# Expert value rows of two token tiles: read as one dense matrix product instead of gathered row by row

## The reference

```
q = xn @ w_q                                   # 8 heads x 2 halves of 128
s1, s2 = scores of each half against 128 keys
top 16 of s1, top 16 of s2, top 16 of their 256 sums -> e = i1*128 + i2   (one of 16384 experts)
g = softmax(top scores)
act = gelu(<u_tab[e], xn>)                     # a row of 2048 of the first table
out = sum over 8 heads x 16 picks of (g * act) * v_tab[e]     # a row of the second table
y = rmsnorm(x + out) * g_final
```

## Time and profile before

| | us |
|---|---|
| runs shown, median of 3 | 4106.34 (4100.68 to 4108.57) |
| the profiled execution, its time | 4110.75 |
| its span, first to last instruction | 4108.9 |
| PE busy / DVE busy / POOL busy | 3168.1 / 2447.8 / 1543.0 |
| mean granted TensorE clock | 0.928 of full |

### The profile page before, as it was taken

The page is one execution under the profiler, slowest core; times in us unless marked ns, Lnnn a source line. Parts: engine busy times, 40 slices in busy tenths (PEclk is TensorE's granted clock), DMA queues, the critical chain, the costliest instruction groups (busy, mean ns, idle before and its releaser), DMA issues.

```text
span 4108.9 us, 35344 instructions
## 1 busy us (share of the span) xinstructions
PE 3168.1 (77%) x11808; PEld 1910.2 (46%) x11808; DVE 2447.8 (60%) x3360; ACT 556.5 (14%) x1113; POOL 1543.0 (38%) x1130
## 2 busy tenths in 40 slices
PE   6999899879878776857915777777777777776776
PEld 5999889775444443535502233232223232322322
DVE  2788810146787775784666565566556555656553
ACT  4444320110010000001000100010011001001100
POOL 2000000014554443552336455445445544554442
PEclk9999999889999998978968999999999999999999
DMA  4322367569999998896879999999999999999997
GB/s 122 89 85 84 104 215 242 190 244 344 391 380 387 385 392 343 333 385 253 342 263 406 409 416 421 421 403 421 414 416 417 422 415 415 418 421 412 422 412 306
DMA packets 406321, 1372.39 MB, mean 334 GB/s; under 512 B 24449, under 2 KB 264065, under 8 KB 264735
## 3 DMA queue, kind: packets, MB, share of 16 engines
q0 software_dynamic: 157584, 1145.05, 68.3%
q1 hardware_dynamic: 246382, 221.85, 16.9%
q10 hardware_dynamic: 2257, 4.40, 0.3%
HBM read 1363.20 MB, written 8.86 MB: 334 GB/s over the span
## 4 chain that ended last, share of the span: by engine, by line
DMA 43%; PE 29%; DVE 14%; issue 9%; POOL 4%; ACT 1%; SPq 0%; DVEq 0%; POOLq 0%; ACTq 0%
DMA region<-in_v_tab_dram,region 29%; DMA region<-in_u_tab_dram,region 13%; PE ps L1366 11%; PE ps L1547 6%; POOL region L527 4%; DVE region L1177 3%; PE ps L1349 3%; PE ps L1351 3%; PE ps L1350 3%; DVE region L1230 2%; DVE region L1168 1%; DVE region L1129 1%; DVE region L1126 1%; DVE region L1128 1%; DVE region L1125 1%
## 5 line engine op out<-in xcount | busy, mean ns | idle before, releaser
L1547 PE MATMUL ps<-region,region 128*128 128x512 f32 x3032 | 1429.1, 621 | 544.0 <-DMA region<-in_v_tab_dram,region 326.8
L1366 PE MATMUL ps<-region,region 128*128 128x160 f32 (+1 forms) x5120 | 1237.2, 404 | 190.4 <-DVE region L1065 57.3
L1230 DVE SCALAR_TENSOR_TENSOR region<-region,region 128x2048 f32<-128x2048 f32 x384 | 876.2, 2291 | 738.8 <-DMA region<-in_u_tab_dram,region 738.8
L527 POOL DMA_INDIRECT region<-in_v_tab_dram,region x544 | 764.3, 1405 | 1268.6 <-PE ps L1547 675.8
L1547 PEld LDWEIGHTS ps<-region,region 128*128 128x128 f32 x3032 | 575.8, 197 | 1397.4 <-issue 1304.3
L1366 PEld LDWEIGHTS ps<-region,region 128*128 128x128 f32 x5120 | 861.1, 196 | 558.9 <-issue 104.1
L527 POOL DMA_INDIRECT region<-in_u_tab_dram,region x544 | 740.7, 1362 | 794.3 <-DVE region L1158 341.0
L1177 DVE SCALAR_TENSOR_TENSOR region<-region,region,region 128x2048 f32<-128x2048 f32 x160 | 376.1, 2351 | 236.8 <-DMA region<-in_v_tab_dram,region 236.6
L1168 DVE SCALAR_TENSOR_TENSOR region<-region,region 128x2048 f32<-128x2048 f32 x160 | 365.3, 2285 | 22.8 <-DMA region<-in_u_tab_dram,region 22.8
L1349 PE MATMUL ps<-region,region 128*128 128x272 f32 x1024 | 297.4, 290 | 0.0
L1351 PE MATMUL ps<-region,region 128*128 128x272 f32 x1024 | 296.4, 289 | 0.0
(11 more groups left out here) (202 smaller groups left out, 1483.2 us busy)
## 6 DMA issues: line engine op xcount, KB each, us to landing
region<-in_w_in_dram SPq DMA_DIRECT2D x192, 512.0 KB
region<-in_w_out_dram SPq DMA_DIRECT2D x64, 512.0 KB
region<-in_w_q_dram SPq DMA_DIRECT2D x64, 512.0 KB
region<-in_w_a_dram SPq DMA_DIRECT2D x32, 512.0 KB
region<-in_w_b_dram SPq DMA_DIRECT2D x32, 512.0 KB
region<-in_u_tab_dram,region POOLq DMA_INDIRECT x544, 14.0
region<-in_v_tab_dram,region POOLq DMA_INDIRECT x544, 14.0
region<-in_x_prompt_dram SPq DMA_DIRECT2D x7, 1024.0 KB, 15.7
```

What stands on the lines that cost most here:

```text
L527: pool.indirect_dma_start(out=slot, out_offset=None, in_=rows_ap, in_offset=bass.IndirectOffsetOnAxis(ap=idx[:, k:k + 1], axis=0)).then_in ...
L1230: stt(out=u_b[s], in0=u_b[s], scalar=1.0, in1=xn_tile(UNITS_A + u), op0=ALU.mult, op1=ALU.mult, accum_out=dots[u % 2][:, k:k + 1]).then_in ...
L1366: last = mm(outs[n][:, 0:WIDTH[g]], wide[s][:, q, n * P:(n + 1) * P], rhs(k), start=(k == 0), stop=(k == n_k - 1))
L1547: last = mm(acc[n][:, b * 512:(b + 1) * 512], diag[:, m, :], v_b[s][:, b * 512:(b + 1) * 512], start=(m == 0), stop=(m == len(rows) - 1))
```

## The change

Group 1's first two tiles (stage 1 of group 1, 256 row steps) gather no value rows. For each token DVE and ACT make one-hot rows from its 128 picks: the upper 7 bits of the expert's number, times the weight (`first_ones`, DVE), and the lower 7 bits (`second_ones`, ACT: 1 - (c - i)^2, cut at 0). PE multiplies the two for one token into a 128x128 block: that token's weights over all 16384 experts. Four tokens are a batch, 32 batches a tile. ACT copies them out of PSUM into `wx` and `wy` (`keep_weights`), 64 KB per partition each. The first tile's batches are spread over the second tile's rows; the second tile's all stand behind 8 row steps of the third. Then SP reads v_tab once, in 128 chunks of 128 rows (1 MB, plain, two slots), and PE multiplies each chunk with both tiles' weights: 8 products of 128x512 per chunk, all accumulated in the 8 banks of PSUM.

The third tile's 128 value rows are gathered and added on DVE, 18 steps behind, while the dense product runs; its u rows then have 2 slots, its value rows 2. Of group 0's 160 value rows, 80 are gathered in its own time and added on DVE, every other step or so; the other 80 are gathered during stage 1, 2 slots, and added on PE by diagonals. The scores of group 1 go to memory and come back unit by unit, since their place is taken. Two memsets at the start (3 and 552 columns) move behind the transposes of the keys, and many regions lie elsewhere. The number of u rows is as before.

```diff
@@ -62,13 +62,25 @@
 ROWS_A = UNITS_A * TOPK
+ROWS_W = 5 * TOPK
+ROWS_1, ROWS_B = 2 * P, 3 * P
 SLOTS_U, SLOTS_V = 3, 2
-TIDY = 19
+VALUE_AT = {V_LAG + v * (ROWS_A - V_LAG) // ROWS_W: v for v in range(ROWS_W)}
+ROWS_P = ROWS_A - ROWS_W
+GROUP_P = 3 * TOPK
+ROW_AT = [m * (ROWS_1 - 2 * TOPK) // ROWS_P for m in range(ROWS_P)]
+BATCH = 4
+BATCHES = P // BATCH
+SPLIT_AT = (P + 4, ROWS_1 + 1)
+BATCH_AT = [[P + 8 + b * (P - 9) // BATCHES for b in range(BATCHES)],
+            [ROWS_1 + 2 + b // 4 for b in range(BATCHES)]]
+ADD_AT = (P + 7, ROWS_1 - 30)
+FOLD_AT, TIDY_AT = ROWS_1 - 26, ROWS_1 - 10
+CHUNKS = 128
+HALF = CHUNKS // 2
+ND = 8
...
@@ -487,13 +513,31 @@
-            for t in range(3):
-                sp.dma_start(xfb[t].rearrange("p (k n) -> p k n", n=P), kept[:, :, t, :]).then_inc(x1_back, 16)
-            sp.dma_start(gfin, g_final.partition_broadcast(P)).then_inc(gfin_in, 16)
+            def kept_rows(t, dst, landed):
+                sp.dma_start(dst.rearrange("p (k n) -> p k n", n=P), kept[:, :, t, :]).then_inc(landed, 16)
+
+            sp.dma_start(gfin[0], g_final.partition_broadcast(P)).then_inc(gfin_in, 16)
+            sp.wait_ge(dot_a, ROWS_A)
+            kept_rows(2, xfz, xz_in)
+            sp.wait_ge(y_ready, 1)
+            sp.dma_start(y_prompt[0, 3 * P:4 * P, :], xf[0]).then_inc(out_p, 16)
+            sp.wait_ge(y_ready, 2)
+            sp.dma_start(xs_out, xf[1][0:TS, :]).then_inc(out_p, 16)
+            sp.wait_ge(v_used, ROWS_P)
+            for c in range(CHUNKS):
+                if c == 1:
+                    sp.wait_ge(built, 2 * BATCHES)
+                if c >= 2:
+                    sp.wait_ge(vt_used, c - 1)
+                sp.dma_start(v_t[c % 2], v_rows[c * P:(c + 1) * P, :]).then_inc(vt_landed[c % 2], 16)
+                if c == HALF + 8:
+                    kept_rows(0, xf[2], xy_in)
+                    kept_rows(1, xf[3], xy_in)
+                    sp.dma_start(gfin[1], g_final.partition_broadcast(P)).then_inc(gfin_again, 16)
+            for n, (row, t) in enumerate(((2 * P, 4), (0, 2), (P, 3))):
+                sp.wait_ge(y_ready, n + 3)
...
@@ -545,47 +591,56 @@
+            def value_row(n):
+                e = n if n < ROWS_A else n + ROWS_1
+                gather(v_rows, v_a[n % SLOTS_V], va_landed[n % SLOTS_V], idx_all, e)
+
+            for p in range(ROWS_A + 1):
                 if p < ROWS_A:
                     if p % TOPK == 0:
                         pool.wait_ge(routed, p // TOPK + 1)
                     if p >= SLOTS_U:
                         pool.wait_ge(dot_a, p - SLOTS_U + 1)
                     gather(u_rows, u_a[p % SLOTS_U], ua_landed[p % SLOTS_U], idx_all, p)
-                v = p - V_AHEAD
-                if v >= 0:
+                if p - 1 in VALUE_AT:
+                    v = VALUE_AT[p - 1]
                     if v >= SLOTS_V:
                         pool.wait_ge(v_added, v - SLOTS_V + 1)
...
+            for r in range(ROWS_1):
+                if r % TOPK == 0:
+                    pool.wait_ge(routed, UNITS_A + r // TOPK + 1)
+                if r == 2:
+                    pool.wait_ge(q_done, 2 * HEADS + 2)
+                if r >= SLOTS:
+                    pool.wait_ge(dot_b, r - SLOTS + 1)
+                gather(u_rows, u_b[r % SLOTS], ub_landed[r % SLOTS], idx_all, ROWS_A + r)
+                for m, at_row in enumerate(ROW_AT):
+                    if at_row == r:
+                        if m < SLOTS_V:
+                            pool.wait_ge(v_added, ROWS_W)
+                        else:
+                            pool.wait_ge(v_used, m - SLOTS_V + 1)
+                        value_row(ROWS_W + m)
+            for z in range(P + V_LAG + 1):
+                if z < P:
+                    r = ROWS_1 + z
+                    if z % TOPK == 0:
+                        pool.wait_ge(routed, UNITS_A + r // TOPK + 1)
+                    pool.wait_ge(dot_b, r - 1)
+                    gather(u_rows, u_b[2 + z % 2], ub_landed[2 + z % 2], idx_all, ROWS_A + r)
+                v = z - V_LAG - 1
+                if v >= 0:
+                    if v < SLOTS_V:
+                        pool.wait_ge(v_used, ROWS_P)
+                    else:
+                        pool.wait_ge(v_added, ROWS_W + v - SLOTS_V + 1)
+                    value_row(ROWS_A + v)
...
@@ -832,13 +894,52 @@
+            def diagonal(m):
+                act.wait_ge(w_ready, (ROWS_W + m) // TOPK + 2)
+                if m >= ND:
+                    act.wait_ge(v_used, m - ND + 1)
+                part(act)
+                nc.scalar.activation(diag[:, m % ND, :], ident, ACT.Copy,
+                                     scale=w_all[:, ROWS_W + m:ROWS_W + m + 1]).then_inc(diag_ready, 1)
+            def second_ones(t, b):
+                n = t * BATCHES + b
+                if n >= 2:
+                    act.wait_ge(built, n - 1)
+                for q in range(BATCH):
+                    last = nc.scalar.activation(one_b[n % 2][:, q, :], count, ACT.Square, scale=-1.0,
+                                                bias=turned[:, 1, BATCH * b + q:BATCH * b + q + 1])
+                last.then_inc(b_square, 1)
+                act.wait_ge(b_square, n + 1)
+                nc.scalar.activation(one_b[n % 2], one_b[n % 2], ACT.Relu, scale=-1.0, bias=ones[:, 0:1]).then_inc(b_ones, 1)
+
+                act.wait_ge(built, n + 1)
+                if t == 0:
+                    nc.scalar.activation(wx[:, :, cols], src, ACT.Copy).then_inc(kept_w, 1)
+                else:
+                    nc.scalar.activation(wy[0][:, :, cols], src[:, 0:HALF], ACT.Copy)
+                    nc.scalar.activation(wy[1][:, :, cols], src[:, HALF:CHUNKS], ACT.Copy).then_inc(kept_w, 1)
...
@@ -866,36 +967,55 @@
             for u in range(UNITS_B):
+                for m, at_row in enumerate(ROW_AT):
+                    if at_row // TOPK == u:
+                        diagonal(m)
+                if u == 2 * HEADS:
+                    turned_copy(1)
+                    act.wait_ge(out_p, 32)
+                    build(1, list(range(BATCHES)))
                 if u < UNITS_B - 1:
                     stage_scores(UNITS_A + u + 1)
                     exponents(UNITS_A + u + 1)
+                if u == HEADS:
+                    turned_copy(0)
+                build(0, [b for b in range(BATCHES) if BATCH_AT[0][b] // TOPK == u])
...
@@ -1220,65 +1343,96 @@
+            def first_ones(t, b):
+                n = t * BATCHES + b
+                dve.wait_ge(turn_read, t + 1)
+                if n >= 2:
+                    dve.wait_ge(built, n - 1)
+                for q in range(BATCH):
+                    col = BATCH * b + q
+                    last = ts_(one_a[n % 2][:, q, :], count, turned[:, 0, col:col + 1], turned[:, 2, col:col + 1],
+                               ALU.is_equal, ALU.mult)
+                last.then_inc(a_ones, 1)
+
...
+            for j in range(2):
+                dve.wait_ge(s_done[j], 2 * HEADS + 1)
+            for r in range(ROWS_B):
+                u, k = divmod(r, TOPK)
+                dot(r)
+                if k == 1:
+                    expert_weights(UNITS_A + u - 1)
+                if k == (12 if u == 2 * HEADS else 3) and u < UNITS_B - 1:
+                    route(UNITS_A + u + 1)
+                    for b in range(BATCHES):
+                        if BATCH_AT[t][b] == r:
+                            first_ones(t, b)
+                if r == ROWS_1 + V_LAG:
+                    dve.wait_ge(xz_in, 16)
+                if r >= ROWS_1 + V_LAG:
+                    value_z(r - ROWS_1 - V_LAG)
+            expert_weights(UNITS_A + UNITS_B - 1)
+            for z in range(P - V_LAG, P):
+                value_z(z)
+            dve.wait_ge(gfin_again, 16)
+            for n in range(2):
+                dve.wait_ge(dense_done, n + 1)
+                tt(xf[2 + n], xf[2 + n], acc[n], ALU.add).then_inc(dense_read, 1)
+            for n in range(2):
+                normalised(slice(2 + n, 3 + n), 6 + n, 1)
...
@@ -1531,28 +1685,71 @@
+            def value_row(m):
+                n = ROWS_W + m
+                first, last_row = m in (0, GROUP_P), m in (GROUP_P - 1, ROWS_P - 1)
+                if m == GROUP_P:
+                    pe.wait_ge(acc_read, 1)
+                pe.wait_ge(diag_ready, m + 1)
+                pe.wait_ge(va_landed[n % SLOTS_V], 16 * (n // SLOTS_V + 1))
+                for b in range(4):
+                    last = mm(acc[0][:, b * 512:(b + 1) * 512], diag[:, m % ND, :],
+                              v_a[n % SLOTS_V][:, b * 512:(b + 1) * 512], start=first, stop=last_row)
+                last.then_inc(v_used, 1)
+
...
+            def batch(t, b):
+                n = t * BATCHES + b
+                if n >= 4:
+                    pe.wait_ge(kept_w, n - 3)
+                pe.wait_ge(b_ones, n + 1)
+                pe.wait_ge(a_ones, n + 1)
+                for q in range(BATCH):
```

(19 more changed lines are left out.)

345 lines of the change are left out of this document (187 added, 158 removed).

## The result

The changed kernel takes 4185.86 us (median, 4177.36 to 4213.84) where the kernel before, beside it on the same chip, takes 4107.45 (4100.68 to 4111.97). The ratio is 1.0204, 95% interval 1.0177 to 1.0231: slower by 2.0%, 78 us; the interval leaves open whether it is a little more or less than 2%. The forecast was 3974, and faster.

What follows compares the result with a forecast made beforehand. From 2203 us on, DMA transfers were the bound. First stretches 1940 + stage 1 928 + weight matrix 128 + dense product 960 + end 20 = 3976 us span, so 3974, 3.2% less; range 3905 to 4050, chance 0.53.

Steps and rivals of the forecast that it cites:

- first stretches: Branch, output product and query product before group 1's third tile: 565, 203 and 184 us, ending at 1940.
- end: After the dense product: last chunk 7 us, then add, squares, root, normalise and output 13 us; 20 in all.
- The formula for a chunk: Dense product, two slots: PE's 6.99 plus 0.8 plus landing 7.4, divided by 2, gives 7.6 us per chunk.
- I take 3 us lost per unit: Stage 1: DMA idles while DVE routes with fewer slots; 52.9 us per 16-row unit becomes 56.
- about half of the engines: Dense product: the plain queue's share beside gathers, so a chunk lands in 5 us plus some 2.4 of start.
- rival (b): Dense loop runs on landing: plain queue gets a third, 9.2 us a chunk, 223 us more, 4197; chance 0.13.
- the gathers, with the other half, need about the same: Dense product: the gather stream takes about as long as the chunks' 972 us, so both end together; 960 taken.
- Wrong if: Signs: chunk over 8.6 us, gather stream ending over 100 us from the dense one, or ACT's batch over 5 us.
- (c): Stage 1 is a chain through four engines: 68 us a unit, 160 us more, 4134; chance 0.09.
- (a): Everything near the DMA rate: stage 1 870, matrix 108, dense 942 us; 3878 in all; chance 0.18.
- (d): First stretches don't shorten, bound by u rows and DVE's order; only 51 us go: 4106; chance 0.07.
- The two rules weighed: DVE's port lock slows gathers, 55 us per stage 1 unit, hardware reads immune; DMA engines alternate between queues by packet.

Runs made afterwards that it cites:

- the two kernels where it doesn't wait: Changed kernel without table reads after two chunks, 4072.68 us; changed kernel without the third tile's gathers after two rows of each kind, 3949.52 us.
- both of its edits: Changed kernel with the third tile's value gather issued ahead of the expert row's and the value table read in halves of a chunk into four half slots: 4075.76 us.
- The seven-slot kernel: Changed kernel with seven slots instead of four for u rows in stage 1, up to row 216: 4128.96 us, ratio 1.0039 to the kernel before.
- the kernel with halves alone: Changed kernel with the value table read in halves of a chunk into four half slots: 4186.93 us.
- all edits: Changed kernel plus value gather first, table halves, four slots for last value rows, seven u slots, second unit's scores copied in place: 3969.36 us, ratio 0.9659.

## Why the prediction was wrong

The sum, term by term (span, us):

| step | predicted | measured | off by |
|---|---|---|---|
| first stretches end at | 1940 | 1927 | -13 |
| stage 1 | 928 | 1018 | +90 |
| second tile's weight matrix | 128 | 100 | -28 |
| dense loop | 960 | 1067 | +107 |
| end | 20 | 70 | +50 |

The differences make 206, and 3976 + 206 = 4182.

**Right.** The first stretches: 576, 193 and 178 us where 565, 203 and 184 were put down. The weight matrix took what its lower end said: 2.7 us a batch (86 / 32), where 2.8 stood. PE per chunk, 894 predicted, 882 to 887 in the two kernels where it doesn't wait. The formula for a chunk. The dense stretch at full engines: 942 us predicted; with both of its edits the loop takes 973 and the rows' stream ends 31 later.

**Stage 1, the step that read "I take 3 us lost per unit".** The text said that while DVE routes, DMA can finish only what lies in the slots, and then charged 3 us for it. A unit's bytes take 52.9 us at the full rate and the unit took 62, so 9 us are lost: four slots hold only four u rows ready when the route ends, and behind these a row takes 3.6 us. The seven-slot kernel, at 55 us a unit, is the 56 that I had put down: the step that failed is the carrying of that rate to four slots. The 4 us for batches in units 8 to 15 (the 9th to 16th) were too much with four slots (1.6 each) and right with seven (these units sum to 488 us with the batches and 458 without, 4 each). The wait for the spilled scores, 20 us in the first unit, was costed as 15 us of transfer for both ways and nothing of waiting; it was missing from the steps.

**Dense loop, the step "about half of the engines".** In 3120 to 4060 the plain queue got 32% of the engines' time and 35% of the bytes, and landings of 9.0 us where 7.4 were put in, so rival (b)'s mechanism is what happened, at 8.3 us a chunk instead of 9.2. The share of half was not misread: in the kernel before the queue has it in 3798 to 3812, 50.3%, while several outputs lie in it. What failed is that two slots of 1 MB were taken to keep the queue like that. A slot has a transfer under way for 9.0 of its 16.7 us, and while both are full or in use the queue is empty; in the kernel with halves alone the four half slots raise its share to 40%, and the loop takes 7.05 us a chunk. Of the evidence on landings, 10.7 us among gathers, too little was kept: 9.0 lies midway between it and 7.4. By the prediction's own account 8.3 us a chunk doesn't make the kernel slower, 8.6 does; it took the other two steps as well.

**End, the step "the gathers, with the other half, need about the same".** They were never worked out as a chain. Their slots, order and landing stood in the diff: 17 us for two rows. The 4.3 us per value row was named as the danger and came true: after the last dot, at 4072, the last 18 rows took 90 us, 5.0 each. Without the table beside them they take 86. In the kernel with both edits they take 93, and 72 once they have four slots: the two slots are the larger cause. Where the three steps meet is one error: from 2203 on the kernel before ran at 416 GB/s with 8 slots of 1 MB, and I carried that rate over to 6 slots. The kernel before with 6 slots shows 320.

**The signs.** None of the three under "Wrong if" came: a chunk took 8.3 us, the streams ended 51 us apart, a batch took 2.7 us. The units of 62 us, where 56 and 60 stood, and the streams' distance, where 30 stood, were what showed the miss; a limit for stage 1 was lacking.

**Rivals.** (b) as above. (c), the chain through four engines: 63.6 us a unit looks like it, but units 2 to 8, which have no batches, take 62 as well, the batches left out gave 13 us, and POOL waited in the whole stage 24 us for PE's value rows and 343 for dots. It is the ring. (a) occurred in no kernel. With all edits the stretches are near the forecast's own: group 1's rows begin at 1932 (1940), stage 1 takes 936 us (928), the matrix 96 (128), the dense loop 986 (960), the end 22 (20). That 3969 is so near to 3974 is in part luck, since the matrix and the dense loop are off in opposite directions; and it is another kernel. (d) didn't occur.

**The two rules weighed.** By the rule on the port pair (the Trainium skill's "SBUF — State Buffer", SBUF: two separate sides) a DVE busy four fifths of the time should slow the gathers. POOL's issues beside a dot do take 2.5 us and not 0.94, here as before. Yet it doesn't limit the rate: with all edits DVE is busy 407 of 500 us and the DMA engines are at 1.00 and 411 GB/s. That plain reads are untouched by DVE, which no run had shown, the kernel without the third tile's gathers shows: 4.9 us a chunk with DVE busy 394 of 400 us, and 4.9 with DVE idle.

What stays open: some 7 of the 15 us between the sum of single edits and all of them; what holds units 9 to 16 at 56 to 66 us with seven slots besides the batches; and whether the table would get more in 8 KB packets with four slots than in 4 KB packets, which was not run.

## What to carry to other kernels

Fewer bytes help only at the rate at which the new slots and the new order of issue can ask for them: for each stream divide the turn of a slot (wait, issue, landing, use) by the slots, add what stands in series with it (here a route) less what the rows that lie ready win back, and take the larger of this and the bytes' time. Take the landing from a stretch with as much under way: it is no constant. When one queue issues two kinds of transfers, put first the one whose slot comes free first. When two queues share full engines, don't give the one that matters shorter packets, and keep a transfer of it under way at all times.

## What was not expected of the hardware

- A landing isn't a property of the transfer: gathers of 1 MB took 15 us with eight slots in turn (416 GB/s), 9.4 with six in stage 1 (358), 7.7 to 8.8 with six in the kernel before (320), and the u rows' 6.1 with four and no table (269).
- Full engines share by packet: 8 KB packets beside 8 KB packets got half while both queues were filled, 4 KB packets a third of the bytes, 2 KB packets a quarter, though alone the 2 KB packets kept up with PE.
- The scores' way to memory, 3 MB from SBUF in one transfer, took 31.2 us from issue to landing while gathers ran; at 416 GB/s its bytes take 7.6.
